# End of a state-space mixer: GELU and lag copies first, weights rounded in the fifth batch, products between the last outputs

## The chip, the cores and the metric

One Trainium2 chip, one of its cores. The time is device microseconds (us) of one execution; the figure for a kernel is the median of its runs.

## The reference, cut to what matters

Two layers run over 528 positions (16 meta tokens and 512 inputs) of width 1024. The first layer's mixer is what the change touches:

```
u = rms_norm(x, ln_mix)                       # 64 groups of 16 channels, 64 complex states each
x_t = Abar x_{t-1} + Bbar u_t                 # diagonal linear recurrence, per group
y_t = Re(C x_t) + d * u_t
g = gelu(y)                                   # (528, 1024)
mix = (g @ w_glu_a) * sigmoid(g @ w_glu_b)    # two products 1024 x 1024
h = h + mix
...                                           # SwiGLU feed-forward, window attention, feed-forward, norm
```

## The kernel before, in words

The kernel is written out engine by engine; each engine runs its own list in order, and semaphores join them. There is no planner: the order is the program's.

**The mixer** works in 8 batches of 8 groups (`BATCHES`, `GB`), numbered 0 to 7 here, with positions in 66 chunks of 8. For a batch, TensorE (PE) turns the injection matrices (`injection`, lines 1350 and 1351, two halves; ACT copies them out in `front`, line 644), multiplies the inputs by them (`additions`, line 1364), and computes the first rows of the block matrix of lags (`lags`, lines 1384 and 1389; ACT copies them in `lags`, line 671). SP's `place_lags` stores these to DRAM (`k_dram`, line 371) and loads them back eight times, shifted, into `k_toep` (line 379). VectorE (DVE) scans the batch's states (lines 1069 to 1081), one batch ahead of PE's `outputs`. GpSimd makes the tables. `outputs` (lines 1403 and 1408, two halves of two pairs of groups) multiplies `k_toep` and the states into banks 6 and 7; it waits for `toep_placed`, `state_ready` and for the GELU of the batch before, which empties those banks. ACT then runs `gelu` (line 677), stores to `y_dram` (`store_outputs`, line 684), loads the result back with features on the partitions into `y_feat` (`load_outputs`, line 693, eight DMAs, two slots), and `round_input` (line 699) rounds it to `glu_high`; DVE's `split_input` (line 1058) makes `glu_low`, the rest. One batch gives one block k of 128 rows of g.

PE's order in iteration b is `additions(b+1)`, `lags(b+1)`, `injection(b+2)` first half, `outputs(b)` first half, `injection` second half, `outputs(b)` second half; iteration 5 ends with `lags(7)`. ACT's order in iteration b is `read_starts(b+2)`, `lags(b+1)`, `load_outputs(b-1)`, `side(b+2)`, `front(b+2)`, `round_input(b-1)`, in iteration 6 two `round_weights` (line 588), and last `gelu(b)` and `store_outputs(b)`.

**The products after it** are written as high times high, low times high and high times low parts, each in two column parts: six matmuls for one k of one tile (`product`, line 1288). I call that a unit. `early_glu` runs k = 0 to 5 for the first two weight tiles, 12 units, behind all outputs; 4 units for k = 6 and 7 follow. Each k waits for its `gt_split`. Then come the two other tiles of the first four, after the sigmoid and a new pair of weight tiles (`w_high` by ACT, `w_low` by DVE, line 889).

Of the kernel before, what the change touches and what calls it, by code (L numbers as in the profile page):

```python
# [26 lines left out]
P = 128  # L27
# [69 lines left out]
def trunk(nc, x, meta_tokens, ln_mix, ln_ffn, lam_re, lam_im, log_dt, b_re, b_im, c_re, c_im,  # L97
          ssm_d, w_glu_a, w_glu_b, w_qkv, b_qkv, sinks, w_o, b_o, w_gate, w_up, w_down, ln_f, out):
    ctx = ExitStack()
    with ctx:  # L100
        def sb(name, shape, dt=F32, scope=ctx, align=32):
            return scope.enter_context(nc.sbuf_tensor(name, shape, dt, align_bytes=align))
# [6 lines left out]
        def sem(name):  # L109
            return ctx.enter_context(nc.semaphore(name))  # L110
# [8 lines left out]
        powers.close()  # L119
        w_high = sb("w_high", [P, 2, KB, P], F32R, align=STREAM_LINE)  # L120
        skip = ExitStack()
        d_diag = sb("d_diag", [2 * GROUP, PAIRS, GROUP], scope=skip)
        skip.close()
        w_low = sb("w_low", [P, 2, KB, P], F32R, align=STREAM_LINE)
# [155 lines left out]
        inj_ready, inj_tr, inj_copied = sem("inj_ready"), sem("inj_tr"), sem("inj_copied")  # L280
        turn_ready, read_ready = sem("turn_ready"), sem("read_ready")
        v_ready, k_ready, k_copied, zeros_made = sem("v_ready"), sem("k_ready"), sem("k_copied"), sem("zeros_made")
        d_ready, state_ready, y_ready, gelu_ready, y_placed, y_stored, bbar_placed = sem("d_ready"), sem("state_ready"), sem("y_ready"), sem("gelu_ready"), sem("y_placed"), sem("y_stored"), sem("bbar_placed")
        gt_rounded, gt_split, pairs_cleared = sem("gt_rounded"), sem("gt_split"), sem("pairs_cleared")
        fine_ready, powers_ready, k_stored, zeros_stored = sem("fine_ready"), sem("powers_ready"), sem("k_stored"), sem("zeros_stored")

# [71 lines left out]
        def _(sp):  # L358
# [52 lines left out]
            for i in range(N_GLU):  # L411
                if i == 1:
                    sp.wait_ge(zeros_made, 1)
                    sp.dma_start(k_dram.rearrange("b r j q t c -> (b r j q) (t c)")[:, 0:(T - 1) * GROUP].rearrange("(p m) n -> p m n", p=P),
                                 k_toep[:, 0, 0:BATCHES, 0:(T - 1) * GROUP]).then_inc(zeros_stored, 16)
                    place_lags(0)
                    for b in range(BATCHES):
                        if b + 1 < BATCHES:
                            place_lags(b + 1)
                if i == 1:  # L420
                    b = BATCHES - 1
                    sp.wait_ge(y_stored, 16 * BATCHES)
                    sp.wait_ge(gt_split, b - 1)
                    for g in range(GB // 2, GB):
                        sp.dma_start(y_feat[g * GROUP:(g + 1) * GROUP, b % 2],
                                     y_dram[b, :, :, g, :].rearrange("s q c -> q s c")).then_inc(y_placed, 16)
                load_tile(i, 0, by_rows(w_glu_b[0])[:, :, 2 * P * i:2 * P * (i + 1)], wait=i > 0)
                load_tile(i, 1, by_rows(w_glu_a[0])[:, :, 2 * P * i:2 * P * (i + 1)], wait=i > 0)

# [150 lines left out]
        def _(act):  # L580
            def round_weights(quad, off, wait=True):

                quad, off = quad + off // 4, off % 4
                slot, j = off // 2, off % 2
                act.wait_ge(raw_loaded[slot], 16 * (quad + 1))
                if wait:
                    act.wait_ge(w_used, 4 * quad + off - 1)
                nc.scalar.copy(w_high[:, j], raw[:, slot, :, j * P:(j + 1) * P]).then_inc(w_rounded, 1)  # L588
# [77 lines left out]
            def lags(b):  # L666

                act.wait_ge(k_ready, b + 1)
                if b >= 2:
                    act.wait_ge(k_stored, 16 * (b - 1))  # L670
                nc.scalar.copy(k_lag[:, b % 2].rearrange("p t c -> p (t c)"), banks[:, 4, 0:P]).then_inc(k_copied, 1)
# [15 lines left out]
            def load_outputs(b):  # L687

                act.wait_ge(y_stored, 16 * (b + 1))
                if b >= 2:  # L690
                    act.wait_ge(gt_split, b - 1)
                for g in range(GB if b < BATCHES - 1 else GB // 2):
                    nc.scalar.dma_start(y_feat[g * GROUP:(g + 1) * GROUP, b % 2],  # L693
                                        y_dram[b, :, :, g, :].rearrange("s q c -> q s c")).then_inc(y_placed, 16)

            def round_input(b):

                act.wait_ge(y_placed, 16 * GB * (b + 1))
                nc.scalar.copy(glu_high[:, b], y_feat[:, b % 2].rearrange("p s c -> p (s c)")).then_inc(gt_rounded, 1)

            read_starts(0)
# [3 lines left out]
            side(0)  # L705
            front(1)
            side(1)
            for b in range(BATCHES):
                if b + 2 < BATCHES:
                    read_starts(b + 2)  # L710
                if b + 1 < BATCHES:
                    lags(b + 1)
                if b >= 1:
                    load_outputs(b - 1)
                if b + 2 < BATCHES:
                    side(b + 2)
                    front(b + 2)
                if b >= 1:
                    round_input(b - 1)
                if b == BATCHES - 2:  # L720
                    round_weights(QUAD_GLU, 0, wait=False)
                    round_weights(QUAD_GLU, 1, wait=False)
                gelu(b)
                store_outputs(b)
            load_outputs(BATCHES - 1)
            round_input(BATCHES - 1)
            def updated(k, m, n, gain):

# [143 lines left out]
        def _(dve):  # L872
# [11 lines left out]
            def split_weights(quad, off):  # L884

                quad, off = quad + off // 4, off % 4
                slot, j = off // 2, off % 2
                dve.wait_ge(w_rounded, 4 * quad + (off + 1))
                nc.vector.tensor_tensor(w_low[:, j], raw[:, slot, :, j * P:(j + 1) * P], w_high[:, j],  # L889
                                        ALU.subtract).then_inc(w_split, 1)  # L890
# [164 lines left out]
            def split_input(b):  # L1055

                dve.wait_ge(gt_rounded, b + 1)
                TT(glu_low[:, b], y_feat[:, b % 2].rearrange("p s c -> p (s c)"), glu_high[:, b], ALU.subtract).then_inc(gt_split, 1)

            make_injection(1)  # L1060
            for b in range(BATCHES):
                pr = slice(b * PB, (b + 1) * PB)
                tr, ti = (turn[:, b % 2, :, i].unsqueeze(1).to_broadcast([P, 2, PB, CS]) for i in range(2))
                v, cross, out = state_banks(), zt[:].rearrange("p i r c -> p i (r c)"), state[:, b % 2].rearrange("p i r c -> p i (r c)")
                v4 = v.rearrange("p i (r c) -> p i r c", c=CS)
                dve.wait_ge(turn_ready, b + 1)
                dve.wait_ge(side_ready, b + 1)
                dve.wait_ge(v_ready, b + 1)
                TT(zt[:], v4, ti, ALU.mult)
                step(TT(v4, v4, tr, ALU.mult))  # L1070
                TT(v[:, 0], v[:, 0], cross[:, 1], ALU.add)
                step(TT(v[:, 1], v[:, 1], cross[:, 0], ALU.subtract))
                for i in range(2):
                    ins = nc.vector.tensor_tensor_scan(v[:, i], flat(decay_row[:, b % 2]), v[:, i], 0.0, ALU.mult, ALU.add)
                step(ins)
                TT(zt[:], v4, ti, ALU.mult)
                step(TT(v4, v4, tr, ALU.mult))
                if b >= 2:
                    dve.wait_ge(y_ready, b - 1)
                TT(out[:, 0], v[:, 0], cross[:, 1], ALU.subtract)  # L1080
                TT(out[:, 1], v[:, 1], cross[:, 0], ALU.add).then_inc(state_ready, 1)

                if b + 2 < BATCHES:
                    make_injection(b + 2)
                if 2 <= b < BATCHES - 1:
                    split_input(b - 2)
            dve.wait_ge(k_ready, BATCHES)
            split_weights(QUAD_GLU, 0)
            split_input(BATCHES - 3)
            split_weights(QUAD_GLU, 1)  # L1090
            split_input(BATCHES - 2)
            split_input(BATCHES - 1)
            dve.wait_ge(read_ready, BATCHES)
# [180 lines left out]
        def _(pe):  # L1274
# [136 lines left out]
                if PB - 1 in pairs:  # L1411
                    ins.then_inc(y_ready, 1)

            def early_glu(off):

                product(QUAD_GLU, off, 0, GLU_EARLY, glu_high, glu_low, 2 * off, L, stop=False, used=False,
                        each=lambda k: pe.wait_ge(gt_split, k + 1))

            for b in range(2):
                for h in range(2):  # L1420
# [4 lines left out]
            for b in range(BATCHES):  # L1425
                if b + 1 < BATCHES:
                    additions(b + 1)
                if b + 2 < BATCHES:
                    lags(b + 1)
                if b + 2 < BATCHES:  # L1430
                    injection(b + 2, 0)
                outputs(b, (0, 1))
                if b + 2 < BATCHES:
                    injection(b + 2, 1)
                outputs(b, (2, 3))
                if b + 2 == BATCHES - 1:
                    lags(BATCHES - 1)
            early_glu(0)
            early_glu(1)
            for k in range(GLU_EARLY, KB):  # L1440
                pe.wait_ge(gt_split, k + 1)
                for off in range(2):
# [218 lines left out]
```

## Time and profile before

| | us |
|---|---|
| median of 3 runs | 1208.82 (1208.35 to 1208.9) |
| the profiled execution | 1210.54 |
| its span, first to last instruction | 1208.4 |
| PE busy in the span | 1144.9 (95%) |
| DVE, ACT, GpSimd busy | 551.6, 410.5, 185.8 |

The profiled execution lies 2.14 us around its span and 1.72 us above the median. The granted TensorE clock is given as a share of full speed, so 1.00 is 2.4 GHz and 0.50 is 1.2 GHz; its mean over the span is 0.986.

### The profile page before, as it was taken

To read this page: it belongs to the slowest core of one execution; us is meant where nothing else is said; L and a number is where in the kernel's file an instruction comes from. 1 tells how busy PE (TensorE), PEld (TensorE's weight loads), DVE (VectorE), ACT (ScalarE), POOL (GpSimd) and SP (SyncE) were. 2 spreads that over 40 slices of the span, in tenths; PEclk is the share of its full clock that TensorE was granted. 3 is DMA by queue.
4 is the path that set the end of the run, shared out by engine and by line. 5 is a ranking of instruction groups with operands and counts; after the bars stand their busy time and mean duration, and the time that the engine had idled before them with its cause. 6 is when DMAs were issued, how large, how long until landed. Compare 5 with 4: busy or idle time off the path is not lost.

```text
span 1208.4 us, 20385 instructions
## 1 busy us (share of the span) xinstructions
PE 1144.9 (95%) x8339; PEld 1029.3 (85%) x8339; DVE 551.6 (46%) x821; ACT 410.5 (34%) x698; POOL 185.8 (15%) x137
## 2 busy tenths in 40 slices
PE   4399889999999999999999989989999999999997
PEld 4388789999999999999999867668888888888886
DVE  5677624554333343334444355455443443434443
ACT  5723222333222222223333355543323232323332
POOL 3979300002111111100000000000211112110000
PEclk9999879999999999999999999999999999999999
DMA  7225422232322323222233311113323332223322
GB/s 134 74 63 104 103 81 95 73 103 71 104 82 92 104 69 104 66 80 80 95 95 105 123 36 36 37 36 105 101 75 102 104 104 85 88 74 96 96 96 90
DMA packets 119385, 104.61 MB, mean 87 GB/s; under 512 B 21868, under 2 KB 117216, under 8 KB 119008
## 3 DMA queue, kind: packets, MB, share of 16 engines
q1 hardware_dynamic: 109544, 99.72, 27.0%
q10 hardware_dynamic: 9792, 4.19, 1.5%
q8 instruction: 36, 0.59, 0.2%
q14 instruction: 13, 0.11, 0.0%
HBM read 98.11 MB, written 5.24 MB: 86 GB/s over the span
## 4 chain that ended last, share of the span: by engine, by line
issue 44%; PE 43%; DVE 4%; DMA 4%; POOL 2%; ACTq 2%; ACT 2%; SPq 0%; POOLq 0%; DVEq 0%
PE banks L1288 40%; DMA y_feat<-y_dram 2%; ACTq L693 2%; POOL gate L566 2%; DMA y_dram<-y_act 1%; DMA raw_c_re<-in_ssm_c_re 1%; PE banks L1408 1%; ACT u_row L623 1%; PE banks L1403 1%; PE banks L1350 0%; PE banks L1351 0%; ACT y_act L677 0%; PE banks L1313 0%; DVE pow_t L974 0%; ACT w_high L588 0%
## 5 line engine op out<-in xcount | busy, mean ns | idle before, releaser
L588 ACT CAST w_high<-raw 128x1024 fp32r<-128x1024 f32 x188 | 197.1, 1049 | 583.3 <-PE banks L1288 583.2
L889 DVE TENSOR_TENSOR w_low<-raw,w_high 128x1024 fp32r<-128x1024 f32 x188 | 230.8, 1228 | 216.8 <-ACT w_high L588 216.8
L1288 PE MATMUL banks<-x_high,w_high 128*128 128x512 f32 (+2 forms) x1184 | 320.8, 324 | 1.0 <-DVE x_low L1103 1.0
L1288 PE MATMUL banks<-x_high,w_low 128*128 128x512 f32 (+2 forms) x1184 | 318.3, 322 | 0.0
L1288 PE MATMUL banks<-x_low,w_high 128*128 128x512 f32 (+2 forms) x1184 | 317.4, 321 | 0.0
L1288 PEld LDWEIGHTS banks<-x_high,w_high 128*128 128x128 f32 x1184 | 198.9, 189 | 19.3 <-issue 2.2
L1288 PEld LDWEIGHTS banks<-x_low,w_high 128*128 128x128 f32 x1184 | 198.7, 188 | 16.1
L1288 PEld LDWEIGHTS banks<-x_high,w_low 128*128 128x128 f32 x1184 | 198.1, 188 | 16.7
L1288 PE MATMUL banks<-a_high,w_high 128*128 128x256 f32 (+2 forms) x528 | 140.4, 320 | 0.0
L1288 PE MATMUL banks<-a_high,w_low 128*128 128x256 f32 (+2 forms) x528 | 140.2, 320 | 0.0
L1288 PE MATMUL banks<-a_low,w_high 128*128 128x256 f32 (+2 forms) x528 | 140.2, 320 | 0.0
L566 POOL TENSOR_TENSOR gate<-gate,rstd_row 128x528 f32<-128x528 f32 (+1 forms) x44 | 79.3, 1802 | 389.9 <-ACT gate L769 389.7
L557 POOL TENSOR_TENSOR rstd<-mean_sq,neg_half 88x6 f32<-88x6 f32 (+1 forms) x4 | 4.7, 1172 | 592.1 <-DVE mean_sq L1130 592.1
L1288 PEld LDWEIGHTS banks<-a_low,w_high 128*128 128x128 f32 x528 | 88.4, 188 | 6.9
L1288 PEld LDWEIGHTS banks<-a_high,w_high 128*128 128x128 f32 x528 | 88.3, 188 | 6.9
L1288 PEld LDWEIGHTS banks<-a_high,w_low 128*128 128x128 f32 x528 | 88.2, 188 | 6.7
L1156 DVE TENSOR_TENSOR prod<-banks,gate 128x528 f32<-128x528 f32 (+1 forms) x44 | 30.8, 699 | 131.7 <-PE banks L1288 131.7
L1150 DVE TENSOR_TENSOR gate<-banks,rstd_row 128x528 f32<-128x528 f32 (+1 forms) x44 | 30.6, 699 | 127.8 <-PE banks L1288 120.0
L1288 PE MATMUL banks<-glu_high,w_high 128*128 128x256 f32 (+1 forms) x256 | 53.6, 291 | 2.2 <-DVE w_low L889 2.2
L1288 PE MATMUL banks<-glu_high,w_low 128*128 128x256 f32 (+1 forms) x256 | 53.2, 289 | 0.0
L1288 PE MATMUL banks<-glu_low,w_high 128*128 128x256 f32 (+1 forms) x256 | 53.2, 289 | 0.0
L1288 PEld LDWEIGHTS banks<-glu_high,w_high 128*128 128x128 f32 x256 | 41.3, 194 | 2.6 <-DVE w_low L889 2.5
(270 smaller groups left out, 1232.5 us busy)
## 6 DMA issues: line engine op xcount, KB each, us to landing
raw<-in_ffn_w_gate SPq DMA_DIRECT2D x22, 1024.0 KB, 5.2
raw<-in_ffn_w_up SPq DMA_DIRECT2D x22, 1024.0 KB, 5.1
raw<-in_ffn_w_down SPq DMA_DIRECT2D x16, 768.0 KB, 4.5
raw<-in_ffn_w_down SPq DMA_DIRECT2D x16, 640.0 KB, 4.4
raw<-in_attn_w_qkv SPq DMA_DIRECT2D x6, 1024.0 KB, 5.0
raw<-in_ssm_w_glu_b SPq DMA_DIRECT2D x4, 1024.0 KB, 5.7
raw<-in_ssm_w_glu_a SPq DMA_DIRECT2D x4, 1024.0 KB, 5.4
k_toep<-k_dram SPq DMA_DIRECT2D x64, 64.0 KB, 2.9
```

What stands on the lines that cost most here:

```text
L557: nc.gpsimd.tensor_tensor(rstd[0:tt, 0:nt], mean_sq[0:tt, 0:nt], neg_half[0:tt, 0:nt], ALU.pow).then_inc(rstd_ready, 1)
L566: nc.gpsimd.tensor_tensor(gate[:, j, a:e], gate[:, j, a:e], rstd_row[:, a:e], ALU.mult).then_inc(gate_scaled, 1)
L588: nc.scalar.copy(w_high[:, j], raw[:, slot, :, j * P:(j + 1) * P]).then_inc(w_rounded, 1)
L623: ins = nc.scalar.mul(u_row[:, i % 2, :, T - 1 - s, :], xt[:, s, i * 256:(i + 1) * 256].rearrange("c (g q) -> c g q", q=GROUP), rstd[0:C, ...
L693: nc.scalar.dma_start(y_feat[g * GROUP:(g + 1) * GROUP, b % 2], y_dram[b, :, :, g, :].rearrange("s q c -> q s c")).then_inc(y_placed, 16)
L889: nc.vector.tensor_tensor(w_low[:, j], raw[:, slot, :, j * P:(j + 1) * P], w_high[:, j], ALU.subtract).then_inc(w_split, 1)
L1150: TT(tokens_of(gate[:, j], n), bank_view(2 * j, n), tokens_of(rstd_row[:], n), ALU.mult).then_inc(pre_ready, 1)
L1156: TT(tokens_of(prod[:, j], n), bank_view(4 + 2 * j, n), tokens_of(gate[:, j], n), ALU.mult).then_inc(up_taken, 1)
L1288: ins = nc.tensor.matmul(banks[:, bank + h, b0:b0 + cn], w[:, j, k, :], xx[:, first_k + k, c0 + base:c0 + base + cn], start=start and k == ...
L1403: nc.tensor.matmul(banks[:, 6 + j, c0:c0 + C], k_toep[:, b % 2, 2 * r_ + j, :], u_state[:, b * GB + 2 * r_ + j, :], start=True, stop=False)
L1408: ins = nc.tensor.matmul(banks[:, 6 + j, c0 + 1:c0 + C], read[hs, b % 3, r_, i, 1:T + 1].rearrange("p t q -> p (t q)"), state[hs, b % 2, i ...
```

## The change

ACT's loop is turned: iteration b begins with `gelu(b-1)` and `store_outputs(b-1)`, then `round_input(b-2)`, which stood ahead of that GELU. The weights' first tile is rounded in iteration 4 and the second in iteration 6; `lags(7)` is copied at the end of iteration 5, before `gelu(5)`. Batches 6 and 7 follow the loop. DVE splits the first weight tile behind the states of batch 6, and `split_input(4)` behind those of batch 7. For that `d_diag`, which `lags` reads until batch 7, now overlays the second half of `w_low` and not the first. SP issues half of the loads of `y_feat` of batch 6 too, and not of batch 7 alone, and `y_placed` is two semaphores, one for each slot. On PE four of the twelve early units move: k = 0 and 1 of tile 0 between the halves of `outputs(6)`, k = 2 behind it, k = 3 between the halves of `outputs(7)`.

```
+        sb("w_low_first", [P, KB, P], scope=skip, align=STREAM_LINE)
         d_diag = sb("d_diag", [2 * GROUP, PAIRS, GROUP], scope=skip)
...                                                              # SP
-                    b = BATCHES - 1
-                    sp.wait_ge(y_stored, 16 * BATCHES)
-                    sp.wait_ge(gt_split, b - 1)
-                    for g in range(GB // 2, GB):
-                        sp.dma_start(y_feat[...], ...).then_inc(y_placed, 16)
+                    for b in range(BATCHES - 2, BATCHES):
+                        sp.wait_ge(y_stored, 16 * (b + 1))
+                        sp.wait_ge(gt_split, b - 1)
+                        for g in range(GB // 2, GB):
+                            sp.dma_start(y_feat[...], ...).then_inc(y_placed[b % 2], 16)
...                                                              # ACT
-                for g in range(GB if b < BATCHES - 1 else GB // 2):
+                for g in range(GB if b < BATCHES - 2 else GB // 2):
...
-            for b in range(BATCHES):
+            for b in range(BATCHES - 1):
+                if b >= 1:
+                    gelu(b - 1)
+                    store_outputs(b - 1)
+                if b >= 2:
+                    round_input(b - 2)
                 if b + 2 < BATCHES:
                     read_starts(b + 2)
-                if b + 1 < BATCHES:
                     lags(b + 1)
+                else:
+                    round_weights(QUAD_GLU, 1, wait=False)
                 if b >= 1:
                     load_outputs(b - 1)
                 if b + 2 < BATCHES:
                     side(b + 2)
                     front(b + 2)
-                if b >= 1:
-                    round_input(b - 1)
-                if b == BATCHES - 2:
+                if b == BATCHES - 4:
                     round_weights(QUAD_GLU, 0, wait=False)
-                    round_weights(QUAD_GLU, 1, wait=False)
+                if b + 2 == BATCHES - 1:
+                    lags(BATCHES - 1)
+            for b in range(BATCHES - 2, BATCHES):
                 gelu(b)
                 store_outputs(b)
-            load_outputs(BATCHES - 1)
+                if b == BATCHES - 1:
+                    round_input(b - 1)
+                load_outputs(b)
+                if b == BATCHES - 2:
+                    round_input(b - 1)
             round_input(BATCHES - 1)
...                                                              # DVE
-                if 2 <= b < BATCHES - 1:
+                if 2 <= b < BATCHES - 2:
                     split_input(b - 2)
+                if b == BATCHES - 2:
+                    split_weights(QUAD_GLU, 0)
+            split_input(BATCHES - 4)
             dve.wait_ge(k_ready, BATCHES)
-            split_weights(QUAD_GLU, 0)
+            split_weights(QUAD_GLU, 1)
             split_input(BATCHES - 3)
-            split_weights(QUAD_GLU, 1)
             split_input(BATCHES - 2)
...                                                              # PE
+                if b == BATCHES - 2:
+                    early_glu(0, 0, 2)
+                if b == BATCHES - 1:
+                    early_glu(0, 3, 4)
                 outputs(b, (2, 3))
                 if b + 2 == BATCHES - 1:
                     lags(BATCHES - 1)
-            early_glu(0)
-            early_glu(1)
+                if b == BATCHES - 2:
+                    early_glu(0, 2, 3)
+            early_glu(0, 4, GLU_EARLY)
+            early_glu(1, 0, GLU_EARLY)
```

## Rows read from the trace of the kernel before

**Rows 1.** Waits of PE over the whole span: us in total, times, longest us.
```profile
PE banks L1403 <- ACT y_act L677: 7.1, 2, 6.2
```
**Rows 2.** Timeline of PE, `additions`: start us, us, engine line operation, idle before.
```profile
94.60 1.20 PE L1364 MATMUL banks<-u_state,inj_T 128*64 128x65 f32 x32
...
104.93 1.20 PE L1364 MATMUL banks<-u_state,inj_T 128*64 128x65 f32 x32
...
116.01 1.20 PE L1364 MATMUL banks<-u_state,inj_T 128*64 128x65 f32 x32 [0.68 <-ACT inj_T L644]
...
126.79 1.20 PE L1364 MATMUL banks<-u_state,inj_T 128*64 128x65 f32 x32 [0.39 <-ACT inj_T L644]
...
138.01 1.20 PE L1364 MATMUL banks<-u_state,inj_T 128*64 128x65 f32 x32
```
**Rows 3.** Timeline of PE, last outputs and first products.
```profile
140.13 0.63 PE L1403 MATMUL banks<-u_state,k_toep 128*128 128x66 f32 x4 [0.91 <-ACT y_act L677]
...
142.46 0.87 PE L1403 MATMUL banks<-u_state,k_toep 128*128 128x66 f32 x4
...
152.64 1.09 PE L1403 MATMUL banks<-u_state,k_toep 128*128 128x66 f32 x4 [6.16 <-ACT y_act L677]
...
161.01 0.81 PE L1288 MATMUL banks<-glu_high,w_high 128*128 128x256 f32 x2
...
167.04 0.40 PE L1288 MATMUL banks<-glu_high,w_low 128*128 128x256 f32 x2
...
175.09 0.40 PE L1288 MATMUL banks<-glu_high,w_low 128*128 128x256 f32 x2
177.74 0.51 PE L1288 MATMUL banks<-glu_high,w_high 128*128 128x256 f32 x2 [2.24 <-DVE w_low L889]
```
**Rows 4.** Timeline of ACT (ACTq: its DMA queue), batches 3 to 7.
```profile
117.90 0.61 ACT L677 ACTIVATE y_act<-banks 128x528 f32<-128x528 f32 x1
...
139.37 0.61 ACT L677 ACTIVATE y_act<-banks 128x528 f32<-128x528 f32 x1
...
142.11 4.20 ACTq L693 DMA_DIRECT2D y_feat<-y_dram  x8
149.46 0.63 ACT L699 CAST glu_high<-y_feat 128x528 fp32r<-128x528 f32 x1 [8.74 <-DMA y_feat<-y_dram]
150.00 1.99 ACT L588 CAST w_high<-raw 128x1024 fp32r<-128x1024 f32 x2
151.89 0.60 ACT L677 ACTIVATE y_act<-banks 128x528 f32<-128x528 f32 x1
...
163.85 1.81 ACTq L693 DMA_DIRECT2D y_feat<-y_dram  x4
167.59 0.63 ACT L699 CAST glu_high<-y_feat 128x528 fp32r<-128x528 f32 x1 [5.85 <-DMA y_feat<-y_dram]
```
**Rows 5.** Timeline of SP's queue (SPq), batch 7's lags.
```profile
140.75 0.34 SPq L371 DMA_DIRECT2D k_dram<-k_lag  x1
144.28 3.62 SPq L379 DMA_DIRECT2D k_toep<-k_dram  x8
```
**Rows 6.** DMA issues, window 97 to 105: KB each, median us to landing.
```profile
k_toep<-k_dram SPq DMA_DIRECT2D x8, 64.0 KB, 3.3
...
k_dram<-k_lag SPq DMA_DIRECT2D x1, 64.0 KB, 1.6
```
**Rows 7.** Timeline of DVE: states of batch 7, last split of the input.
```profile
140.13 0.69 DVE L1069 TENSOR_TENSOR zt<-banks,turn 128x520 f32<-128x520 f32 x1
...
145.29 0.42 DVE L1081 TENSOR_TENSOR state<-banks,zt 128x260 f32<-128x260 f32 x1
...
168.26 0.71 DVE L1058 TENSOR_TENSOR glu_low<-y_feat,glu_high 128x528 fp32r<-128x528 f32 x1 [7.03 <-ACT glu_high L699]
```
**Rows 8.** Windows: busy us (instructions) of PE, PEld, DVE, ACT, POOL; PEclk, DMA share, GB/s.
```profile
139.10:142.50 3.40, 2.49 (x28) 2.13 (x25) 2.93 (x6) 1.15 (x3) 0.00 (x0) 1.00 0.29 102
...
152.70:156.10 3.40, 3.40 (x20) 3.04 (x20) 1.42 (x2) 0.00 (x0) 0.00 (x0) 0.50 0.27 90
```

More of the change, by code:

```diff
@@ L282, in trunk @@
         v_ready, k_ready, k_copied, zeros_made = sem("v_ready"), sem("k_ready"), sem("k_copied"), sem("zeros_made")
-        d_ready, state_ready, y_ready, gelu_ready, y_placed, y_stored, bbar_placed = sem("d_ready"), sem("state_ready"), sem("y_ready"), sem("gelu_ready"), sem("y_placed"), sem("y_stored"), sem("bbar_placed")
+        d_ready, state_ready, y_ready, gelu_ready, y_stored, bbar_placed = sem("d_ready"), sem("state_ready"), sem("y_ready"), sem("gelu_ready"), sem("y_stored"), sem("bbar_placed")
+        y_placed = [sem("y_placed0"), sem("y_placed1")]
         gt_rounded, gt_split, pairs_cleared = sem("gt_rounded"), sem("gt_split"), sem("pairs_cleared")
@@ L420, in _ @@
                 if i == 1:
-                    b = BATCHES - 1
-                    sp.wait_ge(y_stored, 16 * BATCHES)
-                    sp.wait_ge(gt_split, b - 1)
-                    for g in range(GB // 2, GB):
-                        sp.dma_start(y_feat[g * GROUP:(g + 1) * GROUP, b % 2],
-                                     y_dram[b, :, :, g, :].rearrange("s q c -> q s c")).then_inc(y_placed, 16)
+                    for b in range(BATCHES - 2, BATCHES):
+                        sp.wait_ge(y_stored, 16 * (b + 1))
+                        sp.wait_ge(gt_split, b - 1)
+                        for g in range(GB // 2, GB):
+                            sp.dma_start(y_feat[g * GROUP:(g + 1) * GROUP, b % 2],
+                                         y_dram[b, :, :, g, :].rearrange("s q c -> q s c")).then_inc(y_placed[b % 2], 16)
                 load_tile(i, 0, by_rows(w_glu_b[0])[:, :, 2 * P * i:2 * P * (i + 1)], wait=i > 0)
@@ L691, in load_outputs @@
                     act.wait_ge(gt_split, b - 1)
-                for g in range(GB if b < BATCHES - 1 else GB // 2):
+                for g in range(GB if b < BATCHES - 2 else GB // 2):
                     nc.scalar.dma_start(y_feat[g * GROUP:(g + 1) * GROUP, b % 2],
-                                        y_dram[b, :, :, g, :].rearrange("s q c -> q s c")).then_inc(y_placed, 16)
+                                        y_dram[b, :, :, g, :].rearrange("s q c -> q s c")).then_inc(y_placed[b % 2], 16)
             def round_input(b):
-                act.wait_ge(y_placed, 16 * GB * (b + 1))
+                act.wait_ge(y_placed[b % 2], 16 * GB * (b // 2 + 1))
                 nc.scalar.copy(glu_high[:, b], y_feat[:, b % 2].rearrange("p s c -> p (s c)")).then_inc(gt_rounded, 1)
@@ L1412, in outputs, with early_glu @@
                     ins.then_inc(y_ready, 1)
-            def early_glu(off):
-                product(QUAD_GLU, off, 0, GLU_EARLY, glu_high, glu_low, 2 * off, L, stop=False, used=False,
-                        each=lambda k: pe.wait_ge(gt_split, k + 1))
+            def early_glu(off, k0, k1):
+                product(QUAD_GLU, off, 0, k1 - k0, glu_high, glu_low, 2 * off, L, start=k0 == 0, stop=False, used=False,
+                        w_k=k0, each=lambda k: pe.wait_ge(gt_split, k + 1))
             for b in range(2):
```

## The prediction

> **What bounds the kernel now.** I read the waits of PE first, then its timeline around the mixer, then ACT, SP's queue and DVE beside it, and the windows for the clock. PE is busy for 95% of the span, so what is to be had is its idle time and its slow time. The waits show 7.1 us in two waits of `outputs` for a GELU [rows 1]. The timeline says which: 0.91 us before the outputs of batch 6 and 6.16 us before those of batch 7 [rows 3]. Two small ones stand in the loop, 0.68 and 0.39 us before `additions`, for ACT's copy in `front` [rows 2].
>
> ACT's rows tell why the GELUs are late. `outputs(6)` ends some 4.2 us (half of the 8.37 of the low level) behind 142.46, near 146.6, and its GELU starts at 151.89. Ahead of it in ACT's list stood the loads of y(5) (142.11, 4.20 us of issue), the wait of 8.74 us for them to land (`round_input` at 149.46) and 1.99 us of weight rounding [rows 4]. So PE waits for a DMA round trip that it does not need yet.
>
> The second cost is the clock. At the left of 142.5 the granted clock is 1.00; it is 0.50 in the window at 152.7, though PE is busy for all of that window [rows 8]. One half of `outputs` takes 2.33 us at 2.4 GHz (140.13 to 142.46); both halves of batch 7 take 8.37 us (152.64 to 161.01) instead of 4.66. A unit of the early products takes (175.09 - 167.04) / 33 x 3 = 0.73 us at the high level (33 steps of two matmuls lie between these rows), and the 14 steps from 161.01 to 167.04, mostly at the low one, give 1.29 us a unit [rows 3]. From 161.01 all 16 units run without a gap to 175.33, then comes a wait of 2.24 us for the next weights, and behind it PE is nearly always full. What the end of the first 16 units gains is therefore gained by the whole.
>
> **The change, part by part.** I follow the time of each step, at the high clock first.
>
> *GELU first, in the loop.* PE's own round is 104.93 - 94.60 = 10.33 us. The rounds behind it are 11.08, 10.78 and 11.22; the last has 0.89 of `lags(7)` in it, the first two have the idle 0.68 and 0.39 [rows 2]. `gelu(3)` ran at 117.90 though y(3) was ready just before 116.01 - 0.68 = 115.33; it starts then in the changed kernel, and the store and the loads behind it come earlier by some 2 us, so `front(5)` and `front(6)` move up by more than the idle that they caused. The price is that `round_input` (0.63) now stands ahead of the lag copy and that DVE's split comes about 1 us later; DVE needs 5.58 us for a batch's states [rows 7] in a round of 10.33, so I cost it at nothing; without that cover it would be up to 1 us a round. One tile's rounding (1.0 us, half of the 1.99) in iteration 4 lies between `front(6)` and the next y, where the earlier load leaves the room. So the 1.07 us go: `additions(5)` at 115.26, `additions(6)` at 125.59, y(5) ready at 135.92, `lags(7)` done at 136.81, `additions(7)` done at 138.0.
>
> *The lag copy, then GELU 5.* The copy (0.3) follows `lags(7)` to 137.2, `gelu(5)` ends at 137.8, before `additions(7)` does, and the 0.91 is gone: `outputs(6)` starts at 138.0 and not at 140.13, -2.1 us with the 1.07 in it. The GELU could have gone 1.2 us earlier, but PE could not have used it.
>
> *Two units, half, one unit.* 138.0 + 2.33 + 1.46 + 2.33 = 144.1 for y(6), 144.9 with k = 2. The units find their inputs: `split_weights(0)` has stood since the states of batch 6, and k = 0 to 3 were split in the loop. `w_low`'s first half is free, as `d_diag` now lies under the second. The units move and add nothing: 4 x 0.73 = 2.9 us that PE did behind the outputs.
>
> *GELU 6.* ACT's list before it is now `store_outputs(5)`, `round_input(4)`, one rounding, and the issue of the loads of y(5), which start 2.74 us behind `gelu(5)` as before (139.37 to 142.11), at 139.9, and end at 144.1 by the 4.20 of the row. `gelu(6)` runs at 144.2 to 144.8, in time; the landing of y(5) (149.46 - 142.11 = 7.35 us behind the issue) no longer stands before it. This is the 6.16 us.
>
> *What is late next: `k_toep` of batch 7.* SP's store of the lags was issued at 140.75, 0.74 behind the store of y(5), and `k_toep` was asked for 3.53 us later; the landing of such a store is 1.6 us in a quieter round [rows 5, 6]. Now it goes out at 137.25, ahead of `gelu(5)`'s store. The eight loads take 3.62 of issue, less the last one's 0.43, and 3.3 to land: 6.5 us. That gives 145.4 with the 1.6 and 147.3 with the 3.53; from below, they may have landed by 144.7 (PE's turn 144.9) as 3.3 is a median. I take 145.4, since the row with nothing just ahead of the store is the nearer: PE idles 0.5 us. The states of batch 7 are done 5.6 us behind 138.05, at 143.65.
>
> *Batch 7.* 145.4 + 2.33 + 0.73 + 2.33 = 150.8 for y(7), against 161.01. `round_input(5)` (147.3 landed, ACT free from its four issues of y(6) at 148.8) ends at 149.4, before that y. SP's eight waits and issues are behind its `k_toep` loads and ahead only of the next weights, asked for at 165.6 before and near 155.5 now, before DVE needs them. `load_outputs(6)` waits for `split_input(4)`, 0.7 us behind the states, at 144.4; its y is stored at 146.9, so this new order costs nothing, and if the split were late by more than 2.5 us, each us would go to y(6).
>
> *The end.* From y(7) to its split it was 161.01 to 168.97: 7.96 us [rows 4, 7]. `round_input(6)` (0.63) now stands between the store and the loads, in the 2 us in which ACT waits for that store. So k = 7 can start at 158.8; PE has 2 + 6 + 2 units before it, 150.8 + 7.3 = 158.1. Two units more: 160.2. Before it was 175.33. Gain 15.1 us, of which about 2.1 stand at `outputs(6)`, 5.7 in the wait for batch 7, and the rest, 7.3, is the work that ran at 1.2 GHz less the 0.7 us that PE now waits for k = 7. The wait of 2.24 us behind it stays: the new tiles still wait for w_high's slot.
>
> The profiled execution would be 1210.54 - 15.1 = 1195.4, and as the median stands 1.72 us below it, 1208.82 - 15.1 = **1193.7**.
>
> One rule speaks to the clock. The row shows 0.50 for a window in which PE was busy without a gap on `outputs`, and 1.00 at the end of the window 139.10 to 142.50, in which PE was idle for 0.9 us; the fall came right behind it [rows 8]. The Trainium skill (TensorE: Matmul & The Clock Gate, part 1) says that the default state is throttled and that activity releases the throttle. By that rule a PE kept busy from 138.0 on stays at 2.4 GHz, which is my sum; by the row, busy with `outputs` alone is not enough to come back, so a fall would last until the products alone run.
>
> **The rivals.**
>
> *The clock falls at batch 7.* For it: PE had idled 0.91 us some 2 us before the fall, and 0.5 to 2.4 us may stand before `outputs(7)`. Against it: 0.68 us at 116 made no fall, and now products lie between. Price: outputs(7) 8.37 and its unit 1.29 against 5.4, so y(7) at 155.1; then the chain gives 163.1 for the last k, but ten units with the loss of before (14 steps in 6.03 us and not in 14 x 0.244 = 3.4: 2.6) take 9.9 to 165.0, + 1.46 = 166.5. Gain 8.8, **1200.0**. If it falls in the middle of batch 7, some half of the loss: 1196.9.
>
> *It falls at batch 6, as before.* Then 2 + 1.7 us more for the second half and three units: gain 5.1, **1203.7**. The fall before had 0.91 us idle ahead of it, which is gone; so little weight.
>
> *The DMAs are late.* `k_toep` at 147.3 (+1.9), and y(6) lands in 7.35 and not in 3.74 us, which puts `round_input(6)` at 154.9, ahead of the loads of y(7), +1.3. Gain 11.9, **1196.9**.
>
> *Slower.* The clock falls behind the states, and outputs with units strewn between them never bring it back: 138.0 + 2 x 8.37 + 16 x 1.29 = 175.4, just the old end. It decides from there: each further unit in the low state costs 0.56. Before, at most 6.0 us of products alone (161.01 to 167.04) brought it back, and here 12 units are alone. With some six further ones, +3: **1212**.
>
> *It does not do what it says*, since PE is held at a unit by a split or a weight that is late: PE then waits inside `outputs(6)`, and as long as it is under 6 us it is a smaller gain, near **1203**, as the forecast's share of the clock would go with it; nothing in DVE's rows is that late.
>
> **How the numbers follow.** My forecast 50%; clock at batch 7 in whole or in part 24%; late DMAs 12%; clock at batch 6, 5%; held at a unit 4%; slower 3%; 2% for what I do not see. The range goes from 1191.8 (`k_toep` in time, -0.5, and a little in the chain through DRAM, y(6) and y(7) having quieter queues, -1.4) to 1200.4, with the first three cases in it. About 0.2% (2.4 us) is what a measurement of this kernel can tell from no change: faster 0.94, within it 0.03, slower 0.03.
>
> **What would show it.** Right: `outputs(6)` starts at 138, with no wait for `y_act` of over 0.3 us on PE; `gelu(6)` directly behind its y near 144; y(7) near 151; a clock of 1.00 in 142 to 160; the 2.24 us wait near 160.2 and all behind it shifted by 15. Wrong: a clock of 0.50 while batch 7's outputs run; `k_toep` as the wait before them; a wait for `glu_low` of over 1 us before the last units; or idle time that comes back behind 175, if the weights were what the rest waits for.

## The result and the profile after

| | before | changed |
|---|---|---|
| median of 14 runs each, us | 1210.16 (1208.35 to 1214.73) | 1203.5 (1196.26 to 1207.74) |
| ratio to before, 95% interval | | 0.9941 (0.9926 to 0.9956) |
| the profiled execution, its span, its mean clock | 1210.54, 1208.4, 0.986 | 1196.26, 1194.2, 0.995 |

The change gains 6.7 us in the median and not 15.1. The forecast of 1193.7 and the range to 1200.4 missed. The profiled execution is the odd one of the set: 1196.26, where 1195.4 was foretold for it, and every other run took 1201.8 or more. The first trace must therefore be read twice: for the steps, which it bears out, and for what it does not show.

The waits of PE in the window 75 to 200 of the changed kernel (us in total, times, longest), and its timeline:

```profile
PE banks L1302 <- DVE w_low L901: 2.2, 1, 2.2
PE banks L1302 <- DVE glu_low L1070: 1.1, 1, 1.1
PE banks L1417 <- DMA k_toep<-k_dram: 0.6, 1, 0.6
```
```profile
94.23 1.20 PE L1378 MATMUL banks<-u_state,inj_T 128*64 128x65 f32 x32
...
125.21 1.20 PE L1378 MATMUL banks<-u_state,inj_T 128*64 128x65 f32 x32
...
137.56 0.66 PE L1417 MATMUL banks<-u_state,k_toep 128*128 128x66 f32 x4
...
141.50 0.55 PE L1417 MATMUL banks<-u_state,k_toep 128*128 128x66 f32 x4
...
145.37 0.66 PE L1417 MATMUL banks<-u_state,k_toep 128*128 128x66 f32 x4 [0.60 <-DMA k_toep<-k_dram]
...
150.82 0.52 PE L1302 MATMUL banks<-glu_high,w_high 128*128 128x256 f32 x2
...
159.56 0.51 PE L1302 MATMUL banks<-glu_high,w_high 128*128 128x256 f32 x2 [1.15 <-DVE glu_low L1070]
...
160.88 0.40 PE L1302 MATMUL banks<-glu_high,w_low 128*128 128x256 f32 x2
163.52 0.52 PE L1302 MATMUL banks<-glu_high,w_high 128*128 128x256 f32 x2 [2.24 <-DVE w_low L901]
```

Both GELU waits [rows 1] and both waits for `front` [rows 2] are gone; `outputs(7)` starts at 145.37 (145.4 foretold) behind `k_toep`, y(7) is there at 150.82 (150.8). That y(7) hits to 0.02 us is luck: this trace's `additions(3)` starts 0.37 us earlier than before's (94.23 and 94.60), so counted from there y(7) is 0.4 us late. Two halves take 4.7 us and not 8.37 [rows 3]. ACT's and SP's rows in the same trace:

```profile
143.88 0.61 ACT L679 ACTIVATE y_act<-banks 128x528 f32<-128x528 f32 x1 [4.53 <-PE banks L1422]
...
150.94 0.61 ACT L679 ACTIVATE y_act<-banks 128x528 f32<-128x528 f32 x1 [1.83 <-PE banks L1422]
...
153.67 2.20 ACTq L695 DMA_DIRECT2D y_feat<-y_dram  x4
158.13 0.63 ACT L701 CAST glu_high<-y_feat 128x528 fp32r<-128x528 f32 x1 [5.53 <-DMA y_feat<-y_dram]
```
```profile
136.86 0.34 SPq L373 DMA_DIRECT2D k_dram<-k_lag  x1
138.49 4.17 SPq L381 DMA_DIRECT2D k_toep<-k_dram  x8
```

The store of the lags, now ahead of y's, takes 1.6 us and not 3.5 [rows 5, 6]. Whether the order did that is not shown: behind y's store by 0.7 us it took 3.5 us in before's trace and in fill_before's, but 1.65 in gelu6_first's. Two sizes are off. The eight loads of `k_toep` took 4.17 us to issue and not 3.62 [rows 5]. And from the issue of y(7)'s loads to its rounding it is 4.46 us, and 3.74 before [rows 4], so k = 7 starts at 159.56, 0.8 us after 158.8 and 1.1 us late when counted from `additions(3)`.

### The profile page after: what moved, and what is told of

Same layout as the page of the kernel before. It is cut to its first block, busy times and chain, and to the rows that moved or that the text cites. A ratio compares the mean times of both kernels' runs of the same rounds, so it can differ in the third digit from the quotient of the medians.

```text
span 1194.2 us, 20389 instructions
## 1 busy us (share of the span) xinstructions
PE 1137.2 (95%) x8339; PEld 1022.1 (86%) x8339; DVE 553.4 (46%) x821; ACT 410.4 (34%) x698; POOL 185.7 (16%) x137
## 4 chain that ended last, share of the span: by engine, by line
PE 46%; issue 44%; DVE 4%; POOL 2%; DMA 1%; ACT 1%; SPq 1%; POOLq 0%; ACTq 0%; DVEq 0%
PE banks L1302 40%; POOL gate L568 2%; PE banks L1422 1%; PE banks L1364 1%; PE banks L1417 1%; PE banks L1365 1%; DMA raw_c_re<-in_ssm_c_re 1%; ACT u_row L625 1%; PE banks L1378 0%; PE banks L1398 0%; PE banks L1327 0%; SPq L381 0%; DMA k_toep<-k_dram 0%; DVE pow_t L986 0%; DVE fine L989 0%
## 5 line engine op out<-in xcount | busy, mean ns | idle before, releaser
L568 POOL TENSOR_TENSOR gate<-gate,rstd_row 128x528 f32<-128x528 f32 (+1 forms) x44 | 79.2, 1800 | 390.0 <-ACT gate L781 390.0
```

The lines of the kernel that those rows point to most:

```text
L568: nc.gpsimd.tensor_tensor(gate[:, j, a:e], gate[:, j, a:e], rstd_row[:, a:e], ALU.mult).then_inc(gate_scaled, 1)
```

## The experiments

To compare traces whose start-ups differ by up to 3.5 us I use two stretches: E, from the start of `additions(3)` (94.60 in [rows 2]) to the first matmul of the third weight tile (177.74 in [rows 3]), and T, from there to the end of the span. Before: E 83.1, T 1030.7. Changed, first trace: E 69.3, T 1030.7. The table has the median of each kernel's runs (4 to 12 of them); each clock list is the mean granted clock of the runs, sorted. The ratio is to runs of the kernel before from the same set, whose medians go from 1209.4 to 1210.1. E and T are of one trace each.

| kernel | median us | ratio (95%) | mean clock of its runs | E, T of its trace |
|---|---|---|---|---|
| a_again | 1204.4 | 0.9949 (0.9930 to 0.9969) | 0.987 x4, 0.988, 0.990 | 74.4, 1033.3 |
| order_only | 1204.2 | 0.9960 (0.9944 to 0.9975) | 0.986 to 0.990 | 76.6, 1029.6 |
| no_idle | 1202.6 | 0.9942 (0.9921 to 0.9962) | 0.987, 0.988 x2, 0.992, 0.993 x2 | 70.1, 1033.1 |
| dense | 1201.1 | 0.9931 (0.9909 to 0.9952) | 0.990 x3, 0.994, 0.996 x2 | 71.3, 1031.6 |
| fill_before | 1209.1 | 0.9993 (0.9979 to 1.0008) | 0.988 to 0.995 | 79.2, 1030.7 |
| fill_after | 1202.8 | 0.9943 (0.9927 to 0.9958) | 0.988 x3, 0.992, 0.993 x2 | 73.6, 1031.1 |
| dense_fill | 1200.7 | 0.9923 (0.9906 to 0.9941) | 0.993 x5 | 71.0, 1032.9 |
| gelu6_first | 1208.2 | 0.9986 (0.9974 to 0.9999) | 0.983 to 0.989 | 78.6, 1031.2 |
| all_filled | 1197.0 | 0.9884 (0.9863 to 0.9904) | 0.997, 0.998, 0.999 x2 | 70.2, 1028.6 |
| light_filled | 1195.5 | 0.9875 (0.9855 to 0.9895) | 0.998 x3, 0.999 | 69.8, 1028.1 |
| light_again | 1194.9 | 0.9884 (0.9870 to 0.9898) | 0.998 x2, 0.999 x2 | 70.2, 1028.1 |
| rest_filled | 1200.9 | 0.9932 (0.9920 to 0.9944) | 0.991 x2, 0.992, 0.993, 0.994, 0.998 | 75.7, 1028.0 |

**a_again**, the changed kernel unaltered.

> The changed kernel, unaltered. Its profiled execution came at 1196.26 us with the clock at 1.00 through the mixer's end, its other runs at a median of 1203.5. Theory C (clock): in most executions the clock falls to 1.2 GHz somewhere between the outputs of batch 6 and the end of the early products, for 10 to 20 us, and that is the 7 us: a trace with a mean clock of 0.986 to 0.990 shows batch 7's outputs at 8.4 us and not 4.7, and a run's span goes with its mean clock, some 0.5 us for each us spent low. Rival W (landing): the clock is the same, and k_toep or y_feat lands 3 to 7 us later in most executions; then PE idles before outputs(7) or before the last units. Rival E (elsewhere): the mixer's end is as in the first trace (last early unit near 161) and the time is lost behind it. Median 1201 to 1206 in all three.

The trace decides for theory C. Shown are PE's timeline and two windows (busy us of PE, PEld, DVE, ACT, POOL, then the granted clock, DMA share, GB/s):

```profile
147.18 0.66 PE L1417 MATMUL banks<-u_state,k_toep 128*128 128x66 f32 x4 [1.10 <-DMA k_toep<-k_dram]
147.77 1.12 PE L1422 MATMUL banks<-state,read 64*128 64x65 f32 x8
148.82 1.12 PE L1417 MATMUL banks<-u_state,k_toep 128*128 128x66 f32 x4
...
155.39 1.12 PE L1422 MATMUL banks<-state,read 64*128 64x65 f32 x8
```
```profile
147.70:151.10 3.40, 3.40 (x23) 2.97 (x23) 0.65 (x1) 0.63 (x1) 0.00 (x0) 0.51 0.44 80
...
157.90:161.40 3.50, 3.50 (x18) 3.50 (x17) 0.71 (x1) 0.33 (x1) 0.00 (x0) 0.50 0.41 119
```

Up to 147.2 it is the first trace, 1.3 us later from its start-up and 0.5 in the wait for `k_toep`. Then the clock is 0.50 for 13.7 us, the matmuls of a pair of groups take 1.12 us where they took 0.66, and E grows by 5.1. T grows by 2.7: here the clock is low near 260 and for longer near 790 too. Nothing lands 3 us late; rival W falls, and the rival "elsewhere" holds for the smaller part.

**order_only** puts the units back behind the outputs:

```
-                if b == BATCHES - 2:
-                    early_glu(0, 0, 2)
-                if b == BATCHES - 1:
-                    early_glu(0, 3, 4)
...
-            early_glu(0, 4, GLU_EARLY)
+            early_glu(0, 0, GLU_EARLY)
```

> The changed kernel with its orders on ACT, DVE and SP, but all 12 early units of the products again behind the last outputs, none between them. PE then idles some 3 us before outputs(7), waiting for k_toep (142.2 to 145.4). Theory C: the clock falls in nearly all executions, early, and the time is 3 to 6 us above the changed kernel's median, 1205 to 1209; at a clock that stays at 1.00 the units' move is worth little (y(7) 0.7 us earlier, 2.9 us more units behind it): about +1.4 us. Rival W: +1 to +2 us, at 1204 to 1206.

Measured 1204.2, between the changed kernel's two medians (1203.5 and 1204.4): below C's band, within W's. So the number alone speaks for W. The trace speaks for C: PE waited as foretold, and the clock fell at 143.5, 0.3 us into that wait, and was low for 17.1 us. C had set its price too high, as the changed kernel's own median has a fall in it.

```profile
PE banks L1417 <- DMA k_toep<-k_dram: 3.3, 1, 3.3
```

So a gain from the moved units is not shown in the median (0.9960 against 0.9949 and 0.9941, with intervals that overlap); the orders on ACT, DVE and SP carry the change. Trace against trace, E without the moved units is 7.3 us longer than in the first trace, which kept its clock (76.6 against 69.3), and 2.2 longer than in a_again, which lost it too.

**no_idle** and **dense** test what the clock wants: no idle time, or fewer stretches of `outputs` alone.

```
 no_idle: -  early_glu(0, 2, 3)     +  early_glu(0, 2, 4)      # ahead of outputs(7)
          -  early_glu(0, 3, 4)     +  early_glu(0, 4, 5)      # between its halves
 dense:   +  for r_ in range(PB):                              # batches 6 and 7
          +      outputs(b, (r_,))
          +      if b == BATCHES - 2:
          +          early_glu(0, r_, r_ + 1)
          +      elif r_ < PB - 1:
          +          early_glu(*((0, 4, 5), (1, 0, 1), (1, 1, 2))[r_])
```

> The changed kernel with unit k = 3 of tile 0 moved ahead of outputs(7), where PE idled 0.6 us for k_toep, and k = 4 in its old place between the halves of outputs(7). PE has no idle time from 137 to 158 then. Theory C in its form 'a short idle time in batch 7 makes the clock fall': most runs come near the good time, 1196 to 1199. Theory C in its form 'outputs themselves are too thin for the clock, idle or not': as the changed kernel, 1201 to 1205. Rival W: k_toep is later than any unit can cover: as the changed kernel, or 0.7 us less.

> The changed kernel with a unit behind each of the four pairs of groups of outputs(6) (k = 0 to 3 of tile 0) and behind the first three of outputs(7) (k = 4 of tile 0, k = 0 and 1 of tile 1). No stretch of over 1.2 us has outputs alone. At a clock of 1.00 it costs some 1.5 us, since y(7) comes 1.5 us later: 1198. Theory C, thin outputs: the clock stays up in most executions or falls for a shorter time, 1197 to 1200. Theory C, short idle time alone: as no_idle. Rival W: 1.5 us above the changed kernel.

no_idle's median of 1202.6 is where the thin form had it, and not at 1196 to 1199. Its trace keeps 1.00 to 160, but its runs are a split: three of its six lie at 0.992 or 0.993 (1200.2 to 1202.2), three at 0.987 or 0.988 (1203.0 to 1205.7). Taking the idle time away did not hold the clock in all runs; that it held at the mixer's end in the better three is shown for the one with a trace. dense came to 1201.1, above the 1197 to 1200 of the thin form, and three of its six runs were at 0.990. That it is better than no_idle is not shown, as the intervals overlap. Its trace has no low clock before 162 though PE idled 0.49 us ahead of `outputs(7)`; the price is a longer wait for k = 7:

```profile
162.21 0.51 PE L1302 MATMUL banks<-glu_high,w_high 128*128 128x256 f32 x2 [3.03 <-DVE glu_low L1070]
```

**fill_before, fill_after, dense_fill** keep PE busy with matmuls that nobody reads, `filler(n)`, n times 128x128 on `ident`, 0.22 us each at 2.4 GHz.

```
+            def filler(n, bank=4):
+                for _ in range(n):
+                    nc.tensor.matmul(banks[:, bank, 0:P], ident[:], ident[:], start=True, stop=True)
 fill_before: filler(3) ahead of outputs(6), 24 ahead of outputs(7), 7 ahead of the third tile; bank 5
 fill_after:  filler(2) ahead of outputs(7), 4 ahead of k = 7, 7 ahead of the third tile
 dense_fill:  as fill_after on dense, with 9 ahead of k = 7
```

> The kernel before with PE kept busy in its idle times, by matmuls of 128x128 on a constant whose results nobody reads (0.22 us each at 2.4 GHz): 3 ahead of outputs(6), 24 ahead of outputs(7) (5.3 of the 7 to 8 us that it waits there for a GELU), 7 in the wait for the next weights. No order on any engine is changed. Theory C (clock): the clock's fall costs the kernel before 8 us at the mixer's end; with the fillers most executions keep 1.00 from 142 on and the median is 5 to 8 us lower, 1202 to 1205, much as the change reached. Rival W (waits and landings alone set the time): no change or up to 5 us slower, 1210 to 1215, as the fillers move nothing forward.

The gain of 5 to 8 us did not come; the ratio is 1 within its interval, and W's "no change" is what the median did. (The median span is 1.9 us below before's, 1206.2 against 1208.1, with 0.6 us more of device time outside it.) But the test does not speak against the clock as a cost, as the fillers did not hold it. Its windows, and the outputs in PE's timeline:

```profile
138.00:141.80 3.80, 3.80 (x40) 3.39 (x39) 3.69 (x8) 0.00 (x0) 0.00 (x0) 0.98 0.37 100
141.80:148.60 6.80, 6.80 (x35) 6.56 (x36) 1.42 (x4) 1.77 (x3) 0.00 (x0) 0.51 0.65 104
148.60:155.40 6.80, 6.80 (x67) 6.36 (x65) 2.88 (x3) 1.26 (x2) 0.00 (x0) 0.99 0.28 68
155.40:162.20 6.80, 6.80 (x35) 6.58 (x35) 0.71 (x1) 1.14 (x2) 0.00 (x0) 0.51 0.18 54
```
```profile
141.58 1.09 PE L1409 MATMUL banks<-u_state,k_toep 128*128 128x66 f32 x4
...
143.65 7.91 PE L1396 MATMUL banks<-ident 128*128 128x128 f32 x48
151.40 0.56 PE L1409 MATMUL banks<-u_state,k_toep 128*128 128x66 f32 x4
...
154.84 0.72 PE L1409 MATMUL banks<-u_state,k_toep 128*128 128x66 f32 x4
155.50 1.12 PE L1414 MATMUL banks<-state,read 64*128 64x65 f32 x8
```

This is the plainest trace of the study. PE is busy for every microsecond of these windows. The clock falls in the last pair of `outputs(6)`, comes back while the 24 fillers run (each is an fp32 matmul that the profile counts twice, hence x48), and falls again in the last pair of `outputs(7)`, which has nothing else in it. So `outputs` alone can lose the clock with no idle time; the fillers ahead of them only gave it back for a while, and took 7.9 us, nearly 5 of them at the low level.

The same trace corrects another reading. Up to batch 6 this is the kernel before, unaltered, yet PE never waits for `front` here:

```profile
104.36 1.20 PE L1364 MATMUL banks<-u_state,inj_T 128*64 128x65 f32 x32
...
114.68 1.20 PE L1364 MATMUL banks<-u_state,inj_T 128*64 128x65 f32 x32
...
125.01 1.20 PE L1364 MATMUL banks<-u_state,inj_T 128*64 128x65 f32 x32
```

The rounds are 10.3 us each, as in the changed kernel. So the 1.07 us of the two waits in [rows 2] come and go from one execution to the next, and can't be credited to the change from one trace.

> The changed kernel with fillers of the same kind: 2 ahead of outputs(7) (idle 0.6 to 1.1 us for k_toep), 4 ahead of k = 7, 7 in the wait for the next weights. Theory C with 'idle time makes it fall': median 1196 to 1199. Theory C with 'outputs are too thin, idle or not': 1202 to 1204, as the 0.4 us of fillers hardly thicken batch 7. Rival W: 1203.5, unchanged.

As the second form of C has it: 1202.8. Its clock was low for 10.2 us from batch 7 on, though PE had idled only 0.47 us ahead of it, less than the 0.60 of the first trace, which kept its clock. Three of six runs were at 0.988.

> The kernel with a unit behind every pair of the last two batches (median 1201.1, best 1199.8, three of six runs at a mean clock of 0.990) plus fillers: 2 ahead of outputs(7), 9 ahead of k = 7 (it waited 3.0 us there), 7 in the wait for the next weights. Theory C: no thin or idle stretch is left at the mixer's end, so nearly all runs lie at the level of the best, 1198 to 1200. If the falls that are left come from other places (260, 690, 790), median 1200 to 1201. Rival W: 1201, unchanged.

1200.7, five runs within 1.8 us, all at 0.993. The mixer's end of its trace is all at 1.00; its low times are near 257, 693 and 787. The alternative for them holds: they come from other places.

**gelu6_first** is the kernel before with one move:

```
+                if b == BATCHES - 2:
+                    gelu(b)
+                    store_outputs(b)
                 if b >= 1:
                     round_input(b - 1)
```

> The kernel before with one edit: gelu(6) and its store stand ahead of round_input(5) and the two weight roundings, on ACT; nothing else is moved. outputs(7) then waits for k_toep (near 150.2) and not for the GELU (152.6), 2.4 us earlier, and y(6) is stored 4.7 us earlier. Theory C: the clock falls as before, gain 2 to 3 us, 1207 to 1208. Rival W (the wait of 6.16 us is the cost and goes with this edit): 5 to 6 us, 1204.

1.7 us in the median (1208.2, just above C's band; W's 1204 is out). The clock was low for 13.7 us from 148 on, as before. The wait of 6.16 us became one of 4.3 for the next in line:

```profile
150.60 1.12 PE L1407 MATMUL banks<-u_state,k_toep 128*128 128x66 f32 x4 [4.32 <-DMA k_toep<-k_dram]
```

A late GELU hid a late `k_toep`. The lag copy in front of `gelu(5)` alone would not have mended that: order_only has it, and PE still waits 3.3 us for `k_toep`. The moved units fill most of that wait (0.6 us is left).

**all_filled, light_filled, light_again, rest_filled** add fillers where the clock still fell away from the mixer (3 before the last k of the first feed-forward tile, 12 in the wait of 3.0 us at 690, 3 in each of three waits of 1 us near 785; for their banks one semaphore wait of PE is added there, and one is moved behind the 12). light has, in batch 7, a filler behind the first and the third pair and one unit behind the second, and 5 fillers ahead of k = 7; rest has no fillers at the mixer's end. The edit of light on all, and one of the places elsewhere:

```
-                        elif r_ < PB - 1:
-                            early_glu(*((0, 4, 5), (1, 0, 1), (1, 1, 2))[r_])
+                        elif r_ == 1:
+                            early_glu(0, 4, 5)
+                        elif r_ < PB - 1:
+                            filler(1)
...                                                    # transpose_probs
+                if s == 0:
+                    filler(12, 7)
```

> dense_fill (median 1200.7, five runs within 1199.8 to 1201.6, no fall at the mixer's end) with fillers of 0.22 us also in the idle times elsewhere behind which falls of 3.4 to 6.8 us still stood: 3 before the last k of the first feed-forward tile (near 260, idle 1.0), 12 before the first transposed probabilities (near 690, idle 3.0), 3 each in the three waits of 1 us near 785. Theory C: those falls go too, 1.5 us each for three of them: 1196 to 1198, mean clock 0.996 or more. Rival (falls there come from the thin work itself): unchanged, 1200 to 1201.

> all_filled with batch 7 thinner: behind its first and third pair one filler of 0.22 us in place of a unit of 0.73, the unit k = 4 of tile 0 behind the second. y(7) comes 0.9 to 1.0 us earlier and PE waits that much less for k = 7. If this density still holds the clock: 0.8 us below all_filled. If not: some runs fall in batch 7 and the median is 2 to 4 us above it, which tells where between 'a unit in the middle' (the changed kernel, falls nearly always) and 'a unit behind every pair' (never) the clock is lost.

> The changed kernel with fillers only away from the mixer's end: the 3, 12, 3, 3 and 3 of all_filled near 260, 690 and 785. Theory C: the mixer's end still falls in nearly every run (5 to 7 us) and the falls elsewhere are gone (together 3 to 4.5 us, as from dense_fill to all_filled, 3.7): median 1199 to 1200.5. If the median is 1203 or more, the fillers elsewhere are worth nothing by themselves and the gain from dense_fill to all_filled had another cause.

> light_filled again, on another chip or at another time, as its median rested on four runs: 1194.5 to 1197 and a mean clock of 0.998 in all runs by theory C; single runs at 0.990 or less would say that its density is at the edge.

The four went as expected, but for sizes: light_filled gains 1.5 us on all_filled and not 0.8, and rest_filled is 0.4 us above its band. T is 1028.0 to 1028.6 in all four traces, against 1029.6 to 1033.3 without those fillers. In all ten traces without them the clock is low for 3.4 us behind the wait of 3.0 us at 690, in four near 260 and in six near 790 (3.4 or 6.8 us); in these four traces it is low at none of the three. So low clock in T cost 1 to 5 us in the traces of all other kernels here. rest_filled still loses its clock in batch 7 (10.2 us low). It has the changed kernel's order at the mixer's end and no low clock at those three places, so its runs tell most: its trace, with that fall, has a mean of 0.994, four others lie at 0.991 to 0.993, and one is at 0.998, as the kernels with no fall are. By that, five of six executions fell. In light_again the last chain fits:

```profile
146.44 0.66 PE L1423 MATMUL banks<-u_state,k_toep 128*128 128x66 f32 x4 [0.41 <-DMA k_toep<-k_dram]
...
160.53 0.51 PE L1302 MATMUL banks<-glu_high,w_high 128*128 128x256 f32 x2 [0.21 <-DVE glu_low L1070]
164.49 0.51 PE L1302 MATMUL banks<-glu_high,w_high 128*128 128x256 f32 x2 [0.68 <-DVE w_low L901]
```

It is the version that beats both kernels: 1194.9 and 1195.5 in its two sets, 14.5 us below before and 8.0 and 9.5 below the change's two medians; its eight runs lie within 1194.5 and 1196.6. Its medians are near the 1193.7 that the prediction had for a kernel which keeps its clock, but not for the same reasons alone: the fillers in T are in them too.

## Why the prediction was wrong

- *What bounds the kernel:* right. The GELU waits and the low clock were the two costs, and what E gained, T kept (1030.7 in both first traces, with the clock low behind the wait of 3.0 us near 690 and near 790 in both).
- *GELU first, the lag copy, the order on DVE and SP:* right, each to within 0.5 us. Counted from `additions(3)`, `outputs(6)` is 0.1 us early, `outputs(7)` 0.3 and y(7) 0.4 us late. The 1.07 us of waits for `front` are booked as gain without cause, since fill_before's trace lacks them with the old order. The landing in 1.6 us came as chosen, but its reason, nothing just ahead of the store, is not borne out by gelu6_first's 1.65 right behind y's store.
- *What is late next:* right; `k_toep`, 0.6 us in one trace, 1.1 and 1.6 in others (a_again and rest_filled, whose `outputs(7)` starts at 146.28).
- *The end:* mis-sized by 0.8 us, y(7)'s round trip 8.7 and not 7.96 us; with the 0.4 us of y(7), E came to 13.9 less and not 15.1.
- *"One rule speaks to the clock ... a PE kept busy from 138.0 on stays at 2.4 GHz, which is my sum":* **this step failed.** I put the fall down to the 0.91 us of idle time ahead of it, because one trace showed the two together, and gave a fall in batch 7 24% and one in batch 6 5%. Measured, 20 of the 21 executions of the changed kernel whose clock is known (15 of the first set, 6 of a_again) lie at 0.986 to 0.990, and fill_before loses its clock twice without any idle time. In the three traces in which this order of the mixer lost its clock (a_again, fill_after, rest_filled) it was in batch 7. For the runs without a trace this is inferred: no_idle's and dense_fill's traces, with no fall at the mixer's end and the most low clock in T, have a mean of 0.993, so 0.990 or less asks for more. The price in E is 5.1 us in a_again, and with 2.7 us in T a_again comes to 1205.3. The rival that I priced at 1200.0 was nearly the truth, with its fall in the first half of batch 7; it lacked the falls in T and rested on too low a base. It is luck that the measured 1203.5 lies by the 1203.7 of the rival with a fall in batch 6: no trace of the changed order shows that fall.
- *What stays open:* the idle time ahead of `outputs(7)` does not sort these executions (kept with 0.60 us; lost with 1.10, 0.47 and 1.60), and a_again ran the very program of the first trace. What makes one execution in 21 keep its clock is not shown.
- *The base:* the profiled execution and three runs gave 1208.82; fourteen runs give 1210.16. That is 1.3 us of the miss.
- The Trainium skill (TensorE: Matmul & The Clock Gate, part 1) says that activity releases the throttle. The rows agree that it comes back under dense matmuls (the 24 fillers from 143.65 in fill_before, products alone from 161.01 [rows 3]), and differ from my reading of it: a PE with no gap in its busy time lost the clock in stretches where only `outputs` ran. I had the row against that reading in hand [rows 8] and used it for the way back alone, not for the way down.

The gain of 6.7 us is then: 13.9 in E when the clock holds, less 5.1 as it hardly ever does, which is 8.8. The 2.1 us that are left over are not shown: the falls elsewhere differ from run to run (T is 2.7 us longer in a_again), and before's E of 83.1 holds the 1.07 us of waits that not every execution has. Only one run of each kernel has a trace (two of the changed one).

## What to carry to other kernels

Before a sum is made at the high clock, ask of each stretch which matmuls run in it, not only whether PE is busy: here the clock was lost in `outputs` (fp32 matmuls of 128x66 and 64x65) with no idle time, and elsewhere behind waits of 1 and 3 us. Dense work between them in small pieces (a unit or one filler behind every pair, in batch 7 behind all but the last) went with a clock of 1.00 there in all five traces that have it, while one lump of 24 fillers ahead of them did not hold it. Look at the mean clock of all runs, not of one trace, since an execution may be the lucky one in 21. Where a short wait must stay, a few matmuls that nobody reads can fill it: those in T took dense_fill's 1200.7 to all_filled's 1197.0. They are not free everywhere, as the 24 of fill_before gained nothing clear of noise.

## What the runs showed of the hardware

- Two halves of `outputs` took 4.7 us at 1.00 and 8.4 at 0.50, so they follow the clock nearly in full, yet do not hold it. In the kernel before, PE was wholly busy with them from 152.7 to 156.1 at 0.50 [rows 8]; in fill_before it fell to 0.50 at 141.6 and at 155.3, in the last pair of each batch, with PE never idle.
- Behind a wait of 3.0 us near 690 the clock was low for 3.4 us in ten traces of ten, and in none of the four with 12 fillers in that wait.
- The same program had spans from 1194.2 to 1205.6 us in one set of runs, going with the mean clock from 0.995 to 0.986: 11 us between the best and the worst. With fillers it was 1192.5 to 1194.6 at 0.998 or 0.999 in eight runs.
- The store of the lags (64 KB), issued 0.5 us ahead of the store of y, was followed by its loads after 1.6 us (first trace, a_again, order_only). Issued 0.7 us behind it, this took 3.5 us in two traces (before, fill_before) and 1.65 in one (gelu6_first): the order alone does not set it.
